# Modulation by room, rotary passes ahead of the scaling, values at once, and early products of the output projection in a fused two-block diffusion kernel

## The reference, cut to what matters

```python
def layer(x, cx, ...):                            # first block, twice
    mod = c_silu @ ada_w + ada_b
    hx = rmsnorm(x, norm_w) * (1 + scale) + shift
    px = split_cols(hx @ w_in)                    # q, k, v of mixers A, B, C and a gate
    ya = global_gqa(...)                          # 8 heads, rmsnorm of q and k, rotary
    yb = neighbourhood_attn(...)                  # 8 heads, bias by position
    yc_ = window_gqa(...)                         # 8 heads, rotary, sink logit
    ux = jnp.concatenate([ya, yb, yc_], axis=-1) * jax.nn.silu(px[9])
    x = x + gate * (ux @ w_out)                   # the output projection

def _adaln(cvec, w_mod, b_mod, n_chunks):         # second block: 6 chunks of 1024, twice
    m = jax.nn.silu(cvec) @ w_mod[:, :n_chunks * D_MODEL] + b_mod[:n_chunks * D_MODEL]
```

## Time and profile before

| | |
|---|---|
| median of 3 runs | 3038.25 us (3037.64 to 3040.66) |
| the profiled execution's own time | 3042.62 us |
| its span, first to last instruction | 3040.8 us |
| mean granted TensorE clock | 0.980 of full |
| busy share of the span: PE, DVE, ACT, POOL | 94%, 44%, 25%, 6% |
| attention of layer 0, its output projection | 105 to 728 us, 725 to 836 us |
| attention of layer 1, its output projection | 843 to 1376 us, 1376 to 1450 us |

### The profile page before, as it was taken

One profiled execution on the slowest core, in us unless ns is written; L12 is line 12 of the kernel. 1 busy time (PEld: TensorE's weight loads), 2 busy tenths in 40 slices (PEclk: granted clock), 3 DMA queues, 4 the chain that ended last, 5 costly groups with the idle time before them and its releaser, 6 DMA issues.

```text
span 3040.8 us, 33707 instructions
## 1 busy us (share of the span) xinstructions
...
## 2 busy tenths in 40 slices
...
GB/s 283 77 77 73 74 104 70 77 111 114 59 76 139 96 117 99 118 118 125 60 55 56 16 118 329 409 421 421 422 421 206 83 83 228 409 422 421 421 420 288
DMA packets 90672, 586.57 MB, mean 193 GB/s; under 512 B 10193, under 2 KB 10193, under 8 KB 29233
## 3 DMA queue, kind: packets, MB, share of 16 engines
...
...
## 4 chain that ended last, share of the span: by engine, by line
PE 68%; DVE 6%; ACT 1%; issue 1%; DVEq 0%; ACTq 0%
PE BIG L976 45%; PE PJ L976 9%; PE BIG L1748 4%; PE PT L1285 1%; PE PT L1302 1%; PE PT L976 1%; PE BIG L1263 1%; PE PJ L1025 1%; DVE SPILL L2246 1%; PE BIG L1267 1%; PE PT L1724 1%; DVE ARENA L2786 0%; DVE ARENA L2785 0%; PE BIG L1256 0%; PE PT L1704 0%
## 5 line engine op out<-in xcount | busy, mean ns | idle before, releaser
L976 PE MATMUL BIG<-ARENA 128*64 128x512 f32 (+3 forms) x2656 | 552.3, 461 | 4.8 <-DVE ARENA L2808 2.5
L976 PE MATMUL PJ<-HT,W 128*128 128x512 f32 (+2 forms) x1040 | 406.2, 541 | 26.2 <-DVE ARENA L2477 21.4
L976 PEld LDWEIGHTS BIG<-ARENA 128*128 128x128 f32 (+1 forms) x2656 | 290.2, 168 | 253.8 <-issue 224.2
L976 PE MATMUL BIG<-HT,W 128*128 128x512 f32 (+1 forms) x768 | 319.7, 577 | 2.4 <-DVE ARENA L2643 2.1
L976 PEld LDWEIGHTS PJ<-HT,W 128*128 128x128 f32 x1040 | 198.2, 197 | 191.1 <-issue 154.3
L976 PE MATMUL BIG<-W,ARENA 128*64 128x512 f32 (+1 forms) x1280 | 282.0, 573 | 0.9 <-DVE ARENA L2689 0.9
L1959 ACT ACTIVATE ARENA<-PT 128x512 f32<-128x512 f32 (+1 forms) x264 | 145.2, 583 | 474.2 <-PE PT L1285 473.9
L2837 DVE SCALAR_TENSOR_TENSOR XC<-BIG,MOD,XC 128x512 f32<-128x512 f32 x128 | 90.2, 746 | 379.4 <-PE BIG L1748 379.4
L976 PEld LDWEIGHTS BIG<-HT,W 128*128 128x128 f32 x768 | 146.2, 191 | 172.2 <-issue 164.8
L2246 DVE CUSTOM_DVE_ANT_0 SPILL<-W,VEC 128x1024 bf16<-128x1024 f32 x168 | 218.1, 1298 | 21.6 <-DMA W<-in_mod_rows 11.2
L2506 DVE TENSOR_REDUCE STAT<-BIG 128x1 f32<-128x512 f32 (+5 forms) x240 | 169.8, 724 | 42.9 <-PE BIG L1267 37.8
...
## 6 DMA issues: line engine op xcount, KB each, us to landing
ARENA<-in_exp_w SPq DMA_DIRECT2D x168, 1024.0 KB, 18.2
W<-in_exp_w SPq DMA_DIRECT2D x144, 1024.0 KB, 16.9
...
W<-in_mod_rows POOLq DMA_DIRECT2D x128, 512.0 KB, 3.9
...
XC<-in_x POOLq DMA_DIRECT2D x1, 3072.0 KB, 12.0
```

Source lines behind the costliest of these rows:

```text
L976: ins = pe.matmul(out, lhsT, rhs, start=start, stop=stop, skip_group_check=skip)
```

## The change

1. `mod_step` follows a plan instead of a constant rate. Each step adds "room" (3.6 in B, 1.4 in A, 0 in C steps of layer 0; 3.2, 1.8, 0 in layer 1; 0 in the step of A and C pairs that holds rotary passes), and each whole unit places an operation. After operation 55 it pauses for two steps. At most two stand ahead of the scaling; the rest go among the projections. Operations per steps 1-6, 7-12, 13-18, 19-24, 25-48, 49-63, 64, 65-71 of layer 0: 9, 8, 9, 9, 30, 22, 1, 10 before; 22, 21, 17, 16, 26, 0, 0, 0 now. In layer 1, B, A and C steps: 19, 21, 28 before; 42, 21, 0 now (by the same cuts as the stretches of the rows below).
2. In layer 0 the rotary passes stand ahead of the transposes `T2` and the scaling.
3. For B pairs `v_tokens` and `gate` follow `tanh` at once, instead of a step later.
4. Products (0, 0), (1, 0) of the output projection are taken into the last steps, in place of the clock-keeping products, into the banks `PJ`; (1, 1) follows (0, 1) at once.
5. POOL makes the four additions of a unit in one job, at product 3 of the unit before.

```diff
-    first = sum(g < 2 for g, _ in (MOD_ROWS[y] for y, _ in MOD_OPS))
-    late = SECOND_VECTORS if x >= first else 0
-    return late + x * (sum(STEPS) - SECOND_VECTORS - 1) // len(MOD_OPS)
+    return MOD_STEPS[x]
+MODS_ROOM = [{"B": 3.6, "A": 1.4, "C": 0.0}, {"B": 3.2, "A": 1.8, "C": 0.0}]
+def plan_modulation():
+    out, room = [], 0.0
+    pause = 0
+    for layer in range(DEPTH):
+        tiles = STEPS[layer] // len(PAIRS)
+        for n in range(STEPS[layer]):
+            i, t = divmod(n, tiles)
+            at = n + (STEPS[0] if layer else 0)
+            ropes = t == tiles - 2 and i >= 3
+            room += 0.0 if ropes else MODS_ROOM[layer][PAIRS[i][0]]
+            while room >= 1 and len(out) < len(MOD_OPS) and at >= pause:
+                out.append(at)
+                room -= 1
+                if len(out) == MODS_FIRST:
+                    pause = at + 2
+            if at < pause:
+                room = 0.0
+EARLY = [(0, 0), (1, 0), (1, 1)]
+PRODUCT_ORDER = [(0, 1), (1, 1)] + LATE[1:]
...
-    if i == 0:
+    if kind == "B":
         return out + [("v_tokens", i), ("gate", i)]
-    return out + [("next", i)] + ([("gate", i), ("v_tokens", i)] if kind == "B" else [("rope_q", i), ("gate", i)])
+    ropes = [("rope_k", i)] if j == 0 else []
+    return out + [("next", i)] + ropes + [("rope_q", i), ("gate", i)]
...
+    tail = 1 + max(n for n in slots if any(item[0] in ("mm", "vt", "block") for item in slots[n]))
+    for y, item in enumerate(first_products()):
+        slots[tail + y * (last - tail) // len(first_products())].append(item)
...
-            order += [("mod", x) for x in range(len(MOD_OPS)) if mod_step(x) == at]
+            mods = [("mod", x) for x in range(len(MOD_OPS)) if mod_step(x) == at]
+            order += mods[:2]
+            mods = mods[2:]
         todo = list(slots[n])
+        if layer == 0:
+            order += [item for item in todo if item[0].startswith("rope_")]
+            todo = [item for item in todo if not item[0].startswith("rope_")]
...
+        if n >= 0:
+            for y, item in enumerate(mods):
+                todo.insert((y + 1) * len(todo) // (len(mods) + 1), item)
         order += todo
         if n >= 0:
-            if not slots[n]:
+            if not slots[n] and n < tail:
                 order.append(("clock", 2))
...
+            z = (me.units + pair) % 2 * 512
+            x = PJ[pair][:, 0:512] if pair < 2 else big[:, 0:512]
+            return {"X": x, "Y": big[:, 512:1024], "Z": PT[:, z:z + 512]}
...
+                    elif what == "first":
+                        _, pair, k = item
+                        if k == 0:
+                            out_w[pair] = out_units_of(pair)
+                            pe.wait_ge(pj_free[pair], me.pj_uses[pair])
+                            pe.wait_ge(o_read, steps_before + OUT_TILES * (nq // P))
+                        last = mm(PJ[pair][:, 0:nq // 2], out_w[pair][0][:, k, :], U[:, k, 0:nq // 2],
+                                  k == 0, k == OUT_TILES - 1)
```

144 lines of the change are left out of this document (78 added, 66 removed).

## The result

| | median | lowest to highest | runs |
|---|---|---|---|
| before | 3038.42 us | 3037.64 to 3040.66 | 4 |
| changed | 3003.66 us | 2998.94 to 3007.58 | 4 |

The ratio is 0.9884, with a 95% interval of 0.9867 to 0.9901. The change is faster, by 35 us; forecast were 82, in a range of 44 to 104. The time lies above the range.

The account below looks back on a forecast made before the run. The prediction saw TensorE busy for 1058.4 of 1155.3 us, its 97 idle us the room, and modulation badly spread on DVE. Savings of 60.4 us in layer 0 and 23.8 in layer 1, less 2, gave 82: 2956 us, range 2934 to 2994.

Parts of the forecast that it names:

- The long stall: Layer 0's step at the reload of x, where a modulation row lands late: 16.9 becomes 5.5 us, 11.4 saved.
- B1 and B2: First two stretches of layer 0's B pairs: 59 and 58 us instead of 61.3 and 62.3, with 3.5 us allowed.
- signs of being wrong: DVE waiting for rows in B pairs; last steps' clock under 0.9; PE's L2391 or PSUM-read waits over 10 us.
- sign of being right: No wait of PE over 4 us between 105 and 640 us.
- first or third rival: DVE bounds the B pairs (about 2995 us), or the clock falls in the last steps (3001); together 0.22.
- the second rival: Modulation rows come late in B pairs: 1.0 us for each of 80 rows cancels the gain; slower 0.05, same 0.03.
- B pairs: modulations rise from 19 to 42: Layer 1's B pairs: PE stays the bound, a gate or copy may be delayed; 3 us charged.
- The third would be 54: Third stretch of layer 0's B pairs: 60 instead of 67.9 us, as it takes over the second loading of vectors.
- The fourth: Fourth stretch of layer 0's B pairs: loses the rotary wait of 3.3 us and its clock, 60.8 instead of 66.3.
- the steps with rotary passes: Layer 1's A pairs: without modulations in these steps, rotary waits and lower clock go, 10.0 us saved.
- POOL's additions in one piece: Layer 0's units: costs nothing, unless POOL stands before a row load, then up to 5 us a unit.
- the 6 us estimated from that rule: Port collisions in layer 0's four B stretches: some 6 us more DVE work, gain there 14 instead of 20.

Follow-up runs that it names:

- e8: The change with the values of layer 0's second to fourth B pair again at the pair's end, behind the gate; 3028.66 us, ratio 0.9965.
- e10: The change with layer 0's rotary passes behind the scaling again, their steps still without modulation; 3008.86 us, ratio 0.9897.
- e1: The change with a third slot for modulation rows in layer 1, order of work unchanged; 2996.2 us, ratio 0.9859.
- e2: The change with layer 1's rooms B 2.0, A 1.8, C 1.6, so at most two modulations a step; 2982.77 us, ratio 0.9819.
- e12: e11 with layer 0's B room 2.6, C room 0.6, and no modulations in its last two C pairs; 2966.95 us, ratio 0.9763.
- e9: The change with the modulation at the constant rate of the kernel before, second vectors where they were; 3005.44 us, ratio 0.9889.
- e4: The change with layer 1's rotary passes ahead of the gate's projection in A and C pairs; 2999.85 us, ratio 0.9878.
- e5: The change with the edits of e2, e3 and e4 together; 2978.41 us, ratio 0.9797.
- e11: e5 with other rooms: layer 0 B 3.0, A 1.7; layer 1 B 1.8, A 2.0, C 2.0; 2974.34 us, ratio 0.9785.
- e3: The change with POOL's additions of block weights in two jobs again, as in the kernel before; 2997.29 us, ratio 0.9864.
- e6: The change without early output-projection products in the last steps, clock-keeping products there again, projection in plain order; 3012.82 us, ratio 0.9908.

## Why the prediction was wrong

**Right.** The long stall (5.9 against 5.5), layer 0's C pairs and last steps (92.5 and 31.4 against 94.8 and 32), its A pairs, both projections with their new pauses (2.08 us at 714.71 and 2.84 at 1355.63, forecast 2.0 and 2.9), layer 1's last steps, and B1 and B2 with DVE 92% busy. Values at once (e8) and rotary passes ahead (e10) do what was said.

Of the prediction's own signs of being wrong one came: DVE idle in front of modulations, released by the DMA of rows, in B pairs. One sign of being right failed beside it: PE waited 5.50 us at 248.12. The gain of 35 us lies in the span of 20 to 60 that was given 0.22 by the first or third rival, but neither is what happened. B1 and B2 took 59.2 and 57.5 us and not 63 and 60, and the clock of the last steps was 1.00. It was the second rival, late rows, in a milder form than any that it priced.

**Wrong: "B pairs: modulations rise from 19 to 42, DVE from 88.1 to 119 of 205: PE stays the bound, and three modulations in a step may delay a gate or a copy; I charge 3 us."** This is the step with the largest miss, 14.6 us. The gate was delayed as said, but by the wait for a row and not by the modulations' own 1.28 us each. All of layer 1's rows serve one operation, and there are 39 in twelve steps. The average does not show the trouble: they come every 3.7 us (145.7 / 39), and two slots could deliver one in half of 1.28 (operation) + 0.30 (from its end to POOL's issue, 872.46 to 872.76) + 4.5 (landing, counted from the issue), that is every 3.0 us, or every 4.7 when a row lands after 7.9. But a step asks for three or four of them, and the stock is two. The third waits for a load that is issued only when the first is done, and where that load meets a 1 MB load of weights, it takes 7.0 to 7.9 us. The rival that had rows coming late was worked out for layer 0 alone, with an average of 6.8 us a row (at two operations each; layer 0's B pairs had 42 rows, not 38), and rejected by it. e1 gives DVE a third row and gets 8.6 us of this stretch back; e2 asks for no more than two in a step and gets all 17.6. That it is the rows and not the number of modulations is shown by e1, which has the same number, and loses its pause in the one of the three steps where every row is in time. That the rows are late because of the weight loads is read from the times alone; no run moved those.

**Wrong: "The third would be 54 ... 60 instead of 67.9. The fourth ... 60.8 instead of 66.3."** In B3 it is the same again in small: operations 48 to 55 have a row each, at 3.6 a step of 9.5 us one row every 2.6 us, and DVE waited 8.7 us in steps 13 to 15. PE paused for 5.50 us at 248.12, for an output read that stands behind these waits on DVE. The average over layer 0 hid it, since its first 48 operations share 24 rows. In B4 there is no wait for rows. It is 6.1 us longer than in e12, where 11 modulations stand in it instead of 16. Pauses of 1.19, 2.45 and 2.2 to 2.4 us stand in both. New in the change are 2.96 us at 331.88 instead of 0.56, another 1.05, and products at the lower clock behind two of the pauses (2.90 us instead of 1.53 at one place, 3.02 instead of 1.72 at the other). Ahead of the 2.96 us stand a scaling and two modulations that took 1.71, 2.17 and 1.80 us beside additions on POOL, 2.8 us more than their usual 0.35, 1.28 and 1.28. That the forecast's level was about right for fewer modulations is shown: e12 has 59.1 and 62.2, e9 61.1 and 61.1. So what failed for these two stretches is that the added modulations were taken as 10.9 and 9.5 us of DVE work beside PE and nothing more.

**Wrong: "the steps with rotary passes had two modulations (2.7 us) ahead of them and a wait of 2.15 us; ... Three of these and a fourth of 1.5, with 1.1 us of clock each: 10.0".** (These terms add up to 12.4, not 10.0.) Before, the modulations of such a step ran while DVE would have waited for ACT. DVE's rows of before:

```profile
1108.41 1.28 DVE L2246 CUSTOM_DVE_ANT_0 SPILL<-W,VEC 128x1024 bf16<-128x1024 f32 x1
...
1111.06 0.08 DVE L2246 DVE_READ_ACCUMULATOR2_ANT MOD<- 128x1 f32 x1
1111.06 0.16 DVE L2389 RECIPROCAL STAT<-STAT 128x1 f32<-128x1 f32 x1
...
1111.97 0.62 DVE L2391 TENSOR_SCALAR ARENA<-ARENA,STAT 128x768 f32<-128x768 f32 x1
```

In the change DVE is idle for 2 us at that place, as its row in such a step shows, and the rotary wait is 1.78 instead of 2.15:

```profile
1121.63 0.16 DVE L2453 RECIPROCAL STAT<-STAT 128x1 f32<-128x1 f32 x1 [2.02 <-ACT ARENA L2012]
```

The wait is the chain behind the exponential: scaling, gate, rotary passes. An order in which the passes come a step earlier removes it (e4), the modulation's leaving did not. So A pairs gained 1.8 and not 10 us, and C pairs 5.9 instead of 9.0. With rows on time the A pairs take 151.2 us (e1 and e2), 4.2 less than this profile of the change and 1.8 to 2.4 less than four others with late rows; with the passes earlier as well they take 150.1 (e5). The forecast's 147.2 came in no run, the shortest being e11's 148.4; in e4 and e5 PE waits 2.40 us for the normalization (L2423 in e4) instead.

**Smaller.** POOL's additions in one piece were charged with nothing and cost some 4 us (e3). In the last steps of layer 0 seven pairs of clock-keeping products at 1.8 us are 12.6 and not 12.0; the forecast of 32 was met all the same, and by e6 the early products themselves are worth only 1.4 us there.

**The port rule.** In B1 a modulation took 2.76 us and one addition beside it on POOL 1.96, where they take 1.28 and 1.10 otherwise. DVE's row:

```profile
113.14 2.76 DVE L2310 CUSTOM_DVE_ANT_0 SPILL<-W,VEC 128x1024 bf16<-128x1024 f32 x1
```

POOL's rows:

```profile
113.53 1.28 POOL L972 TENSOR_TENSOR ARENA<-W 128x512 f32<-128x512 f32 x1
114.89 1.96 POOL L974 TENSOR_TENSOR ARENA<-ARENA,W 128x512 f32<-128x512 f32 x1
```

The first addition has its usual length. The modulation is longer by about the length of that addition, and the second addition by 0.9 us, until the modulation is done: they go one after the other. Ten of the 76 modulations in layer 0's B stretches passed 1.4 us, by 5.9 us together; before, none of the 35 did. The Trainium skill (SBUF — State Buffer, "Who interferes with whom") says that a VectorE instruction with two SBUF inputs contends with a GpSimd instruction that reads SBUF. The trace agrees, and the 6 us estimated from that rule was the measured size. In the sum it had only a share of the 3.5 us allowed in B1 and B2, because 35 operations had shown none of it. But only three of the 35 overlapped an addition at all, each of them begun 0.6 us or more ahead of it, while 12 of the 76 do so now. The long scalings that the prediction took for the same rule do stand beside additions (0.98 to 1.59 us), but a scaling reads one tile and a 128x1 scalar, so that they are not an example of it.

Behind the last output the changed kernel's profile is 3.0 us longer, although its second projection is 1.0 us shorter. From there to the end the 14 profiled kernels lie between 1660.9 and 1669.4 us, the one before at 1664.8 and the changed at 1667.8, so this is within what differs from one profiled kernel to the next, and no effect of the change.

What stays open: whether moving the weight loads away from the rows would give the 17.6 us back, which no run tried, and why e1's A pairs in layer 0 were longer.
